# First expert's rows as products with a scaled slot matrix, a router of four chunks side by side, and another order of VectorE's and ScalarE's steps

## The reference, cut to what matters

```python
x = x + mix @ w_out[l]
h = rmsnorm(x, g_ffn[l])
x = x + moe(h, w_router[l], b_router[l], w1[l], b1[l], w2[l], b2[l])
# in moe, xt = h as (512, 1024):
logits = (xt @ w_router + b_router).astype(jnp.float32)
top_val, top_idx = lax.top_k(logits, TOP_K)          # 4 of 32
gates = jax.nn.softmax(top_val, axis=-1)
# each expert e gets the rows of its tokens:
act = clamped_swiglu(xb @ w1[e] + b1[e])             # (., 1024) @ (1024, 2048)
y = act @ w2[e] + b2[e]                              # (., 1024) @ (1024, 1024)
# y times its gate is added to its token's row
```

## Time and profile before

| | us |
|---|---|
| median of three runs (lowest to highest) | 1217.55 (1217.22 to 1218.1) |
| the profiled execution, its own time | 1215.54 |
| its span, first to last instruction | 1213.9 |
| TensorE busy in the span | 1164.6 (96%) |
| VectorE, ScalarE, GpSimd busy | 307.9, 190.6, 180.0 |
| read from memory, written | 442.73 MB, 15.12 MB |

### The profile page before, as it was taken

How to read it: one execution, slowest core, us unless ns; L and a number is a source line. 1 busy time by engine, 2 the same in 40 slices (tenths; PEclk the granted TensorE clock), 3 DMA queues, 4 the chain that set the end, 5 groups by cost and what they waited for, 6 DMA issues and landing times. The chain is left out here.

```text
span 1213.9 us, 16524 instructions
## 1 busy us (share of the span) xinstructions
PE 1164.6 (96%) x7077; PEld 479.7 (40%) x7077; DVE 307.9 (25%) x492; ACT 190.6 (16%) x378; POOL 180.0 (15%) x251
## 2 busy tenths in 40 slices
PE   8999999999999999999999999999999999999980
PEld 5877786333333333333333333333333333333330
DVE  6588667321111111111111111111111111111117
ACT  5443612100110100001100000110000011000002
POOL 5300000521211111110111111111111101111000
PEclk9999997899999999999999999999999999999995
DMA  9602665999999999999999999999999999999986
GB/s 326 218 1 85 241 250 199 308 379 426 423 429 425 426 425 426 427 427 426 425 426 424 427 426 427 427 424 426 426 427 427 423 427 424 427 423 428 427 366 250
DMA packets 52236, 454.40 MB, mean 374 GB/s; under 512 B 13108, under 2 KB 14404, under 8 KB 27488
## 3 DMA queue, kind: packets, MB, share of 16 engines
q1 hardware_dynamic: 43760, 433.90, 86.3%
q0 software_dynamic: 7664, 17.05, 3.7%
q10 hardware_dynamic: 736, 2.36, 0.5%
HBM read 442.73 MB, written 15.12 MB: 377 GB/s over the span
## 5 line engine op out<-in xcount | busy, mean ns | idle before, releaser
L927 PE MATMUL ps<-ring_a,blockT 128*64 128x512 f32 x1088 | 240.5, 595 | 4.6 <-DMA ring_a<-in_w 4.6
L1415 DVE TENSOR_SCALAR glu_c<-ps 128x768 f32<-128x768 f32 (+1 forms) x32 | 26.9, 842 | 785.6 <-PE ps L934 497.0
L927 PEld LDWEIGHTS ps<-ring_a,blockT 128*64 128x64 f32 x1088 | 75.3, 137 | 159.0 <-issue 146.6
L953 PE MATMUL ps<-ring_a,actT 128*64 128x512 f32 x608 | 136.7, 596 | 0.0
L1894 POOL DMA_INDIRECT scores<-h_rows,slots x29 | 31.1, 1074 | 487.3 <-PE ps L885 486.4
L1704 ACT ACTIVATE blockT<-ps 128x512 f32<-128x512 f32 x29 | 17.3, 597 | 542.7 <-PE ps L885 542.7
L927 PE MATMUL ps<-ring_b,blockT 128*64 128x512 f32 x384 | 85.1, 595 | 3.1 <-DMA ring_b<-in_w 3.1
L1910 POOL DMA_INDIRECT expert_rows<-normed,slots x32 | 32.7, 1021 | 269.1 <-ACT normed L1733 268.8
L934 PE MATMUL ps<-ring_a,blockT 128*32 128x512 f32 x608 | 72.4, 615 | 0.0
L953 PEld LDWEIGHTS ps<-ring_a,actT 128*64 128x64 f32 x608 | 41.7, 137 | 76.1 <-issue 74.2
L927 PEld LDWEIGHTS ps<-ring_b,blockT 128*64 128x64 f32 x384 | 26.6, 137 | 57.7 <-issue 52.0
(11 more groups left out here) (328 smaller groups left out, 1255.1 us busy)
## 6 DMA issues: line engine op xcount, KB each, us to landing
ring_a<-in_w SPq DMA_DIRECT2D x116, 2048.0 KB, 32.2
ring_b<-in_w SPq DMA_DIRECT2D x38, 2048.0 KB, 30.9
ring_d<-in_w SPq DMA_DIRECT2D x19, 2048.0 KB, 35.0
ring_c<-in_w SPq DMA_DIRECT2D x19, 2048.0 KB, 33.6
ring_a<-expert_rows SPq DMA_DIRECT2D x16, 512.0 KB, 18.4
ring<-in_w_in SPq DMA_DIRECT2D x8, 768.0 KB, 20.3
X<-in_x SPq DMA_DIRECT2D x8, 512.0 KB, 6.3
ring<-in_w_out SPq DMA_DIRECT2D x8, 512.0 KB, 4.9
```

The source lines that it names most:

```text
L927: ins = mm(ps[half * HALF:(half + 1) * HALF, b, :], x_of(k)[0], ring(r)[:, 0, at + half * 512:at + (half + 1) * 512], start=False, stop=(k ...
L953: ins = mm(ps[half * HALF:(half + 1) * HALF, bank, :], actT[:, s % 2 * W2_K + j, s // 2 * HALF:(s // 2 + 1) * HALF], ring(r)[:, 0, j * D + ...
L1415: v.tensor_scalar(width(glu_c, big), width(ps_glu, big), LIMIT, None, ALU.min).then_inc(glu_ready, 1)
```

## The change

- *Router.* The weights of the product are now the router's matrix (128x32) and the tokens move (128 columns). Four chunks are put side by side in four column tiles of the array, two rounds into one bank at column 128 (`PARTS_AT`), so that the 128 partitions hold four partial sums of 32 logits. ACT copies them (`keep_parts`), and a second product with four stacked identities (`stacked`, made by GpSimd) adds the parts and turns them (`logits`).
- *First expert.* Its rows are no longer gathered. `place` makes, for expert 0, `first_pick(t)`: one-hot of token by slot, times the token's norm factor. TensorE multiplies each chunk of `X` with it (`pick_rows`, 8 products a tile into banks 6 and 3), and ACT copies the eight chunks to `rowsT` with the gain as scale (`gain_chunk`, one more small load). `fetch(0)`, the first `turn_block` and the token sums of expert 0 go.
- *Order.* VectorE: `second_norm(2)` and `(3)` stand after the last `place`; the reciprocal is a step of its own (`norm_scale`). ACT: `store_h2(2)` and `(3)` stand after `gate_exp`. TensorE: the sort's sums, the overflow sums and the third expert's token sums are called inside the first product, after chunks 2, 4 and 6; the fillers stand elsewhere and use other operands. SP: slot 12 is loaded with slots 4 and 10. GpSimd: `fetch(1)` no longer waits for the first turn.

```diff
@@ SP
             sp.wait_ge(oproj_done, 2 * TB)
-            load_first(4, 10)
-            sp.wait_ge(rows_in, fetches(0))
-            load_first(12)
+            load_first(4, 10, 12)
             sp.wait_ge(logits_done, TB)
             load_w2(0, 0, w2_slot(0, 0))
@@ TensorE
...
-                logits = ps[:, LOGIT_BANKS[t % 2], 0:E]
+                bank = LOGIT_BANKS[t % 2]
                 for k in range(KT):
-                    ins = mm(logits, xnT[:, k, t * P:(t + 1) * P], w_rt[:, k, :],
-                             start=(k == 0), stop=(k == KT - 1))
-                ins.then_inc(logits_done, 1)
+                    g = k % 4
+                    if k == 4:
+                        pe.wait_ge(h2T_b, t + 1)
+                    ins = mm(ps[g * E:(g + 1) * E, bank, PARTS_AT:PARTS_AT + P], w_rt[:, k, :], xnT[:, k, t * P:(t + 1) * P],
+                             start=(k < 4), stop=(k >= 4), tile_position=(0, g * E))
+                ins.then_inc(parts_done, 1)
+
+            def logits(t):
+
+                pe.wait_ge(parts_ready, t + 1)
+                mm(ps[:, LOGIT_BANKS[t % 2], 0:E], logit_parts, stacked[:, :], start=True, stop=True).then_inc(logits_done, 1)
...
-            out_proj(3, 1, lambda: router(1))
+            out_proj(3, 1, lambda: (logits(0), router(1)))
             turn_h2(2)
+            logits(1)
+            keep_busy(3)
+            turn_h2(3)
             rank(0)
+            keep_busy(2)
+            router(2)
             rank(1)
-            turn_h2(3)
-            router(2)
             router(3)
-            pe.wait_ge(biases_ready, 2)
-            pe.wait_ge(cur_ready, 2)
-            keep_busy(2)
+            logits(2)
+            logits(3)
+            keep_busy(4)
+
+            def pick_rows(t, chunks=range(KT)):
+
+                pe.wait_ge(first_pick_ready, t + 1)
+                for k in chunks:
+                    by_chunk = X[:, t, :].rearrange("p (s q j) -> p s j q", j=2, q=P)
+                    ins = mm(ps[:, PICK_BANKS[k // 4], k % 4 * MANY:(k % 4 + 1) * MANY], by_chunk[:, k // 2, k % 2, :], first_pick(t),
+                             start=(t == 0 and k % 4 == 0), stop=(t == TB - 1 and k % 4 == 3))
+                return ins
+
+            pe.wait_ge(negtop_ready, 3)
+            pick_rows(0)
             rank(2)
-            keep_busy(4)
+            pick_rows(1)
             rank(3)
             keep_busy(3)
-
-            pe.wait_ge(pick_ready, 2 * TB)
...
+            pick_rows(2)
+            pick_rows(3).then_inc(rows_turned, 1)
...
             w1_bias(BIG[0], 0)
-            keep_busy(8)
-            pe.wait_ge(sort_ready, 1)
...
+                amid = {}
+                if i == 0:
+                    amid = {2: order_sums, GROUP: overflow_sums, GROUP + 2: third_sums}
+                elif i == 1:
+                    amid = {GROUP: lambda: turn_act_of(0)}
...
-            turn_block(0)
             expert_blocks(compute)
@@ VectorE
-            dve.wait_ge(small_in, 16 * 9)
+            dve.wait_ge(small_in, 16 * 10)
...
             def second_norm(t):
-                dve.wait_ge(std2_ready, t + 1)
                 if t >= 2:
                     dve.wait_ge(h2_stored, 16 * t)
-                then(v.reciprocal(stat[:, H_R + t:H_R + t + 1], stat[:, H_STD + t:H_STD + t + 1]))
...
                 for t in range(first, end):
-                    for e in range(2):
-                        v.tensor_scalar(pick[:, e, t, :], iota_r[:, :], own_rank[:, t, e:e + 1], None, ALU.is_equal).then_inc(pick_ready, 1)
+                    v.tensor_scalar(first_pick(t), iota_r[:, 0:MANY], own_rank[:, t, 0:1], stat[:, H_R + t:H_R + t + 1],
+                                    ALU.is_equal, ALU.mult).then_inc(first_pick_ready, 1)
+                for t in range(first, end):
+                    v.tensor_scalar(pick[:, 1, t, :], iota_r[:, :], own_rank[:, t, 1:2], None, ALU.is_equal).then_inc(pick_ready, 1)
...
             turned_h2(1)
-            second_norm(2)
+            norm_scale(2)
             select(0)
-            select(1)
             residual(3, 1)
             turned_h2(2)
+            select(1)
+            turned_h2(3)
+            norm_scale(3)
             place(0, 2)
-            turned_h2(3)
-            second_norm(3)
             select(2)
             select(3)
             place(2, 4)
+            second_norm(2)
+            second_norm(3)
@@ ACT
             turned_h2(1)
-            store_h2(2)
+            keep_parts(1)
             turned_h2(2)
             squares_h2(3)
             turned_h2(3)
-            store_h2(3)
+            keep_parts(2)
+            keep_parts(3)
             for t in range(TB):
                 gate_exp(t)
+            store_h2(2)
+            store_h2(3)
...
-                if isinstance(i, int) and i < PICKED:
+                if isinstance(i, int) and i == 0:
+                    for k in range(KT):
+                        ins = a.activation(rowsT[:, k, :], ps[:, PICK_BANKS[k // 4], k % 4 * MANY:(k % 4 + 1) * MANY], ACT.Copy,
+                                           scale=gain_chunk[:, k:k + 1])
...
-            act.wait_ge(h2_stored, 16 * TB)
+            act.wait_ge(small_in, 16 * 10)
             turned_rows(0, BIG[0])
@@ GpSimd
             pool.wait_ge(tok_ready, 1)
-            fetch(0)
-            pool.wait_ge(rows_turned, 1)
             fetch(1)
```

More of the change, by code:

```diff
@@ L63 @@
 PICKED = 3
+PICK_BANKS = (6, 3)
+PARTS_AT = 128
 OVF_W = 4
@@ L232, in layer_kernel, with first_pick @@
         w_out_hi = ring1_r[:, KT // 2 * SLOT:].rearrange("p (c j n) -> p c j n", c=KT, j=2)
+        def first_pick(t):
+            if t < 2:
+                return slots[:, :, :, :].rearrange("p b e w -> p (b e w)").bitcast(F32)[:, t * MANY:(t + 1) * MANY]
+            return w_rt[:, :, :].rearrange("p k e -> p (k e)")[:, (t - 2) * MANY:(t - 1) * MANY]
+        logit_parts = slots[:, :, :, :].rearrange("p b e w -> p (b e w)").bitcast(F32)[:, 2 * MANY:2 * MANY + P]
         cur_token = slots[:, LIST_BLOCKS, 0:2, 0:1]
@@ L374, in fetches @@
         def fetches(upto):
-            return 16 * sum(2 if BIG[i] and i >= STATIC else 1 for i in range(upto + 1))
+            return 16 * sum(2 if BIG[i] and i >= PICKED else 1 for i in range(1, upto + 1))
         def scatters(parity, upto):
@@ L1226, in residual, with norm_scale @@
                                        in1=xt, op0=ALU.mult, op1=ALU.add).then_inc(x2_half, 1)
+            def norm_scale(t):
+                dve.wait_ge(std2_ready, t + 1)
+                then(v.reciprocal(stat[:, H_R + t:H_R + t + 1], stat[:, H_STD + t:H_STD + t + 1]))
             def second_norm(t):
-                dve.wait_ge(std2_ready, t + 1)
                 if t >= 2:
                     dve.wait_ge(h2_stored, 16 * t)
-                then(v.reciprocal(stat[:, H_R + t:H_R + t + 1], stat[:, H_STD + t:H_STD + t + 1]))
                 by_pair = normed[:, t % 2, :].rearrange("p (s j q) -> p j s q", j=2, q=P)
@@ L1683, in store_h2, with keep_parts @@
                 act.dma_start(h2_tiles[t, :, :], normed[:, t % 2, :]).then_inc(h2_stored, 16)
+            def keep_parts(t):
+                act.wait_ge(parts_done, t + 1)
+                if t == 0:
+                    act.wait_ge(list_written, 16)
+                else:
+                    act.wait_ge(logits_done, t)
+                a.activation(logit_parts, ps[:, LOGIT_BANKS[t % 2], PARTS_AT:PARTS_AT + P], ACT.Copy).then_inc(parts_ready, 1)
             load_sqrt()
@@ L1828, in _ @@
                 then(keep_unless_zero(expert_sel[:, :], -s * E, [[-1, E]], 1, 1.0))
+            then(g.memset(stacked[:, :], 0.0))
+            for s in range(4):
+                then(keep_unless_zero(stacked[:, :], -s * E, [[-1, E]], 1, 1.0))
             g.iota(iota_e[:, :], [[1, E]], base=0, channel_multiplier=0, allow_small_or_imprecise_dtypes=True)
```

56 lines of the change are left out of this document (35 added, 21 removed).

## The result

The changed kernel takes **1230.49 us** (median; 1228.27 to 1230.84) beside 1217.38 us for the kernel before on the same chip: a ratio of 1.0103, 95% interval 1.0089 to 1.0117. It is slower by 13.1 us. The forecast was 1230.0, its range 1214 to 1236. The profiled execution has a span of 1226.6 us.

A forecast was written before the change was run, and what follows sets the result against it. The weight stream sets the end from about 282 us, TensorE the pace before. First product 3 us later, overflow copy at 238.0, turn +16.0, stream +12.4: 1217.55 + 12.4 = 1230.0 us, range 1214 to 1236.

The forecast's parts named there:

- Start: First product on TensorE starts at 218.1 us, 3 us later than before, held by the landing of store 2.
- my term: Landing of store 2 of the normalised rows beside the weight loads: 9.6 us, between 2.9 light and 10.2 behind all loads.
- the range that I had named as a sign: Sign in the profile after that the forecast is right: first product at 216 to 219 us, at half clock.
- By the parts alone: Without the added store wait, the shortened parts up to ACT's eight copies would start the first product at 208.7 us.
- The clock: TensorE idles before the first product, starts it at half clock until 235 us; overflow copy done at 238.0.
- the clock comes back at once: Rival, 19%: same chain, but the first product is at half clock for 4 us or never; 1222 to 1224 us.
- Slower still: Rival, 10%: clock low through the whole first product and no transfer quicker; overflow copy at 241.7, total 1236 us.
- The list: List of slots begins at 238.0 us, takes the 52.1 of before less 2 for lighter small transfers.
- The turn: Turn of the second expert's activations follows VectorE's 4.7 us after the list: 292.8 us instead of 276.78, +16.0.
- The stream: Weight load goes out at 297.9 us on an empty queue, lands 7.7 later at 305.6 instead of 293.15: +12.4.
- The light store: Rival, 10%: store 2 lands in 2.9 us, start at 211.4, no fall of the clock; 1215 to 1217 us, no change.
- Faster: Rival, 14%: store light and the list's small transfers light too, 8 us less, list under 47 us; 1214 us.

The follow-up runs named there:

- e1: Changed kernel with one semaphore per buffer for the stores of normalised rows: 1216.82 us, ratio 0.9999 to the kernel before.
- e2: Changed kernel with the overflow sums asked for together with the sort's sums, the store wait kept: 1223.34 us, ratio 1.0048 to the kernel before.
- e6: Changed kernel with SyncE holding back the load of slot 12 and the one behind until the third store lands: 1219.87 us, 1.0028 of before.
- e7: Changed kernel with the fourth store of normalised rows behind ACT's eight scaled copies instead of ahead: 1227.57 us, ratio 1.0100 to the kernel before.
- e3: Changed kernel with both one store semaphore per buffer and the overflow sums right behind the sort's: 1211.26 us, ratio 0.9954 to the kernel before.
- e10: Changed kernel with one store semaphore per buffer, early overflow sums and a late chunk-gains load: 1210.73 us, ratio 0.9949 to the kernel before.
- e4: Changed kernel with 46 filler products ahead of the first product's bias: 1228.75 us, a single time without a ratio.
- e9: Changed kernel with the small load of chunk gains issued later, on a semaphore of its own: 1230.42 us, a single time without a ratio.

## Why the prediction was right, and where its working was not

The mechanism was right in its main links, and e1, e2, e6 and e7 show them: store beside loads, VectorE's wait, the late sort and copy, the list, the turn, the stream. Two links were read wrongly (what the turn waits for, and the queue that the load meets), and one term was 6 us too large. That 1230.0 came out beside 1230.49 is luck: four others were too small, by 6.6 us together.

| step | forecast | measured in after | difference |
|---|---|---|---|
| first product starts | 218.1 | 219.70 | +1.6 |
| from there to the end of the overflow copy | 19.9 | 14.01 | -5.9 |
| from there to the list | 50.1 | 51.03 | +0.9 |
| from there to the turn | 4.7 | 6.40 | +1.7 |
| turn to the landing of the load | 12.8 | 15.2 | +2.4 |
| landing of the load | 305.6 | 306.3 | +0.7 |

- *Start.* The place ended at 204.2 (203.8), the store was sent at 205.65 (205.3) and landed in 10.1 us (9.6): after 3.4 us without a packet it took turns with the loads, where my term had it wait behind them. The start is 0.7 us past the range that I had named as a sign. The eight copies took 1.96 us, 0.245 each; I had put each between 0.11 and 0.3, and chosen 0.17. By the parts alone I had the start 16.8 us behind the out-projection (208.7 less 191.9); e1 shows 17.8. The output projection's end at 192.1 (191.9) came out right by accident: the small load costs nothing that can be told, the router is worth 2.2 and not 1.75, and executions differ by themselves by more than either.
- *The clock: the step that failed.* I read how long the clock had stayed low (199 to 219) and stretched the product over as much. The price stood in my own rows: before, the first product's 32 instructions took 9.22 us and the next ones 7.09, a loss of 2.1 us, with the clock at 0.50 ahead of it there too. In after it is 2.36. The rival "the clock comes back at once" was right about the clock: it put the copy's end 13.7 us behind the start, and 14.0 came. Its time, 1222 to 1224, was too low by the other four terms. "Slower still", with the clock low through the whole product, fell together with my forecast: the clock was back at 1.00 by 226. The Trainium skill (TensorE: Matmul & The Clock Gate, Part 1: The HAM clock gate) says that activity releases the throttle; this trace agrees, with 0.50 while TensorE idled, 0.63 while the product began, 1.00 from 226 on. The trace of before bears it out only in part: 0.50 from 199 to 219, with 18.68 us of work, and that stretch is what misled me.
- *The list.* I had taken 2 us off for lighter transfers. From the end of the copy it takes 49.9 to 52.7 us in after and its variants, beside 52.1 and 51.3 in the two profiles of before, so there was hardly a discount to take.
- *The turn.* I let it follow VectorE's list. In after it follows TensorE: GpSimd's fetch for the third expert stands behind the scatters, which moved with the list, so TensorE waited 5.44 us for it, the clock fell again, and the second product's first half took 5.86 us instead of 3.65. I had asked of each step that the change moves who waits for it, but not of the fetch, which isn't moved itself and is queued behind steps that come later.
- *The stream.* I took the queue to be empty when the load goes out. It landed 10.1 us after its issue, not 7.7: the load sent at 291.5 was still ahead of it and landed at 301.2, and the share was 0.99 from 290 to 300.
- *The other rivals.* The light store (e6: 2.6 us) gives 1.0028 of before, where I had it between 0.998 and 1.0; the store landed at 209.6 and took most of the loss with it, but the clock fell there too (TensorE still waited 3.23 us, then sixteen instructions took 5.10). "Faster" rested on a list of under 47 us, which no kernel shows (49.9 at the least). e3 and e10 are faster by another way: no wait, and the overflow sums early.

## What to carry to other kernels

A part that becomes shorter brings nothing while its consumer, or something its consumer needs next, stands in an in-order queue behind a wait: follow every engine that the result passes through, and look at what each has queued ahead. One semaphore that counts several stores makes a buffer wait for a store that never touched it, and loads that are let out earlier make that store land later. Price such a store by packets: beside loads of larger packets it gets as many as they, and so a small part of the bytes. And price a fallen clock by the rows of the work it slows, not by how long it stayed low; before a difference of 1 or 2 us between two profiles is given a cause, look at a second profile of the unchanged kernel.

## What the runs showed of the hardware

- A store of 512 KB on ScalarE's queue lands in 2.6 us alone and in 9.6 to 12.4 us beside 2 MB loads on SyncE's, within some 1.2 us of the load that was last in the other queue when it was issued (1.1 ahead in after, 0.8 ahead and 0.7 behind in e1, 0.3 behind before). Beside the loads it moves no packet for 3.3 to 3.8 us (0.8 alone, in e6), then one for each packet of theirs (107 beside 106 in after from 209 to 214, 83 beside 83 in e7 from 210 to 214), at a fifth of the bytes.
- A fall of the clock ahead of or in the first product cost it 1.4 to 2.6 us (sixteen instructions in 5.10 to 6.20 us instead of 3.65), behind 10.8 us of idling in after and 3.2 us in e6 alike; fillers that ended 2.6 us ahead of it (e4) left 1.7 us of that.
- A scaled copy of 128x96 by ScalarE takes 0.245 us, an unscaled one of 128x384 0.435: four times the elements for 1.8 times the time.
- The landing of the small loads at the start moves between executions without a change in the code ahead: by 3.0 us between e9 and e10 (56.65 and 53.64), by 1.5 us between the two profiles of before (53.84 and 55.31). The end of the output projection differs by 2.4 and 1.6 us in the same pairs.
